# Where the last four h2 tiles are scaled: in front of the routing, or behind the item table

## The reference

```python
x = x + g1[:, None, :] * mix                       # "x1"
h = modulate(rms_norm(x, norm2_w), sh2, sc2)       # "h2"
idx, gw = grouped_route(h, w_router, router_bias)  # 2 of 32 experts a token
y = routed_experts(h, idx, gw, w_gate, w_up, w_down)
x = x + g2[:, None, :] * y
return rms_norm(x, final_norm_w)
```

## Time and profile before

| what | us |
|---|---|
| median of 3 runs | 3030.65 |
| lowest and highest of them | 3027.68 and 3041.57 |
| span of the profiled execution | 3041.9 |
| PE busy in it | 2759.4 (91%) |
| DVE busy | 2356.1 (77%) |
| ACT busy | 1565.1 (51%) |
| POOL busy | 548.3 (18%) |

### The profile page before, as it was taken

How to read it: one execution, slowest core, us unless ns; L and a number is a source line. 1 busy time by engine, 2 the same in 40 slices (tenths; PEclk the granted TensorE clock), 3 DMA queues, 4 the chain that set the end, 5 groups by cost and what they waited for, 6 DMA issues and landing times.

```text
span 3041.9 us, 34857 instructions
## 1 busy us (share of the span) xinstructions
PE 2759.4 (91%) x12582; PEld 2240.1 (74%) x12582; DVE 2356.1 (77%) x1894; ACT 1565.1 (51%) x1510; POOL 548.3 (18%) x432
## 2 busy tenths in 40 slices
PE   2799999999999788999965999999999999999992
PEld 2577777777677566788864888778888877887872
DVE  4879989987857575444445999889999888988894
ACT  6322222222122653333323877777888777777773
POOL 0000000000211110100001333222343222423230
PEclk8899999999999698999986999999999999999996
DMA  9733333334856426555536899999999999999997
GB/s 326 264 111 104 97 104 97 104 104 132 277 187 198 156 80 233 176 190 181 203 97 240 348 374 365 361 378 375 384 368 372 381 377 378 373 373 369 371 388 278
DMA packets 243520, 781.30 MB, mean 257 GB/s; under 512 B 27713, under 2 KB 122065, under 8 KB 173949
## 3 DMA queue, kind: packets, MB, share of 16 engines
q1 hardware_dynamic: 198738, 615.29, 53.0%
q0 software_dynamic: 34144, 130.08, 14.0%
q10 hardware_dynamic: 10570, 35.05, 3.0%
HBM read 738.30 MB, written 87.11 MB: 271 GB/s over the span
## 4 chain that ended last, share of the span: by engine, by line
PE 31%; DMA 12%; DVE 7%; SPq 5%; issue 4%; ACT 3%; DVEq 0%; POOL 0%; ACTq 0%; POOLq 0%
DMA wraw<-in_w_up_dram 8%; SPq L1514 4%; PE ps L1572 4%; PE ps L1570 4%; PE ps L1571 4%; PE ps L1768 3%; PE ps L1770 3%; PE ps L1769 3%; DVE wlo L1590 3%; PE ps L1870 2%; PE ps L1871 2%; PE ps L1875 2%; ACT whi L1580 2%; DMA wraw_o<-in_w_out_dram 2%; PE ps L1559 1%
## 5 line engine op out<-in xcount | busy, mean ns | idle before, releaser
L1590 DVE TENSOR_TENSOR wlo<-wraw,whi 128x2048 fp32r<-128x2048 f32 x444 | 1003.7, 2285 | 101.9 <-ACT whi L1580 101.6
L1580 ACT ACTIVATE whi<-wraw 128x2048 fp32r<-128x2048 f32 x444 | 848.2, 1918 | 311.5 <-PE ps L1572 91.3
L1570 PE MATMUL ps<-whi,xhi 128*128 128x512 f32 x1184 | 476.7, 403 | 4.5 <-DVE wlo L1590 4.4
L1572 PE MATMUL ps<-whi,xlo 128*128 128x512 f32 x1184 | 464.6, 392 | 0.0
L1571 PE MATMUL ps<-wlo,xhi 128*128 128x512 f32 x1184 | 462.9, 391 | 0.0
L715 PE MATMUL ps<-hh,wih 128*128 128x512 f32 x1056 | 336.9, 400 | 6.3 <-DVE wil L703 6.3
L715 PE MATMUL ps<-hl,wih 128*128 128x512 f32 x1056 | 330.4, 394 | 0.0
L715 PE MATMUL ps<-hh,wil 128*128 128x512 f32 x1056 | 329.9, 393 | 0.0
L1049 DVE SCALAR_TENSOR_TENSOR acc<-u,vcur,acc 128x1024 f32<-128x1024 f32 x240 | 308.3, 1284 | 8.0
L1570 PEld LDWEIGHTS ps<-whi,xhi 128*128 128x128 f32 x1184 | 224.1, 189 | 49.7 <-DVE wlo L1590 7.5
L1572 PEld LDWEIGHTS ps<-whi,xlo 128*128 128x128 f32 x1184 | 222.8, 188 | 48.6
(11 more groups left out here) (375 smaller groups left out, 4300.8 us busy)
## 6 DMA issues: line engine op xcount, KB each, us to landing
wraw<-in_w_gate_dram SPq DMA_DIRECT2D x148, 1024.0 KB, 8.5
wraw<-in_w_up_dram SPq DMA_DIRECT2D x148, 1024.0 KB, 11.8
wraw<-in_w_down_dram SPq DMA_DIRECT2D x148, 1024.0 KB, 10.9
wm<-in_w_mod_dram POOLq DMA_DIRECT2D x88, 512.0 KB, 4.1
wraw_i<-in_w_in_dram SPq DMA_DIRECT2D x72, 512.0 KB, 4.7
wraw_o<-in_w_out_dram SPq DMA_DIRECT2D x128, 256.0 KB, 3.5
wmA<-in_w_mod_dram SPq DMA_DIRECT2D x54, 512.0 KB, 5.4
u<-in_w_mod_dram POOLq DMA_DIRECT2D x24, 512.0 KB, 4.6
```

The costliest lines, as they stand in the source:

```text
L1570: pe.matmul(dst, xhi[:, t, :], whi[:, s, w], start=(t == 0), stop=False)
L1572: last = pe.matmul(dst, xlo[:, t, :], whi[:, s, w], start=False, stop=(t == KT - 1))
L1580: act.activation(whi[:, spl(m), :], wraw[:, raw(m), :], ACT.Copy).then_inc(s_whi, 1)
L1590: dve.tensor_tensor(wlo[:, spl(m), :], wraw[:, raw(m), :], whi[:, spl(m), :].bitcast(F32), ALU.subtract).then_inc(s_wsp[raw(m)], 1)
```

## The change

The four h2 scales move from in front of the routing chain to behind `itab`. POOL's adding stores of them move behind the x1 stores, the clearing of `xrow` and the bias add. SP waits for the x1 stores instead of for the h2 stores, and loads `gp` ahead of the four weight pieces instead of behind them. No instruction is added or taken away, except that SP's four waits name other semaphores.

```diff
@@ block.sync
                     load_piece(sp, 0, GATE, 0, 0)
                     load_piece(sp, 0, *STREAM[0], 1)
                     for j in range(HT, TT):
-                        sp.wait_ge(s_h2s[j], 16)
-                    for m in range(1, NRAW - 1):
-                        load_piece(sp, 0, *STREAM[m], m + 1)
+                        sp.wait_ge(s_x1[j], 16)
                     sp.wait_ge(s_h2p, 16 * HT)
                     sp.wait_ge(s_gst, 32)
                     for h, src in enumerate((modp_d[CHUNKS - 1, :, :], modg_d[:, :])):
                         sp.dma_start(gp[:, 1024 * h:1024 * h + 1024], src).then_inc(s_gp, 16)
+                    for m in range(1, NRAW - 1):
+                        load_piece(sp, 0, *STREAM[m], m + 1)
                     sp.wait_ge(s_tab, 1)
@@ block.gpsimd
-                    pool.wait_ge(s_h2p, 16 * HT)
-                    for j in range(HT, TT):
-                        pool.wait_ge(s_hs, 2 * HT + j - HT + 1)
-                        pool.dma_start(h2_d[j * P:(j + 1) * P, :], h2_tile(j), accum_op=ALU.add).then_inc(s_h2s[j], 16)
                     for j in range(HT, TT):
                         x1_store(j)
                     for j in range(TT):
                         pool.wait_ge(s_x1[j], 16)
...
                     pool.wait_ge(s_gp, 32)
                     pool.dma_start(gp[0:1, :], b_mod[:, 5 * D:6 * D], accum_op=ALU.add).then_inc(s_gb, 16)
+                    pool.wait_ge(s_h2p, 16 * HT)
+                    for j in range(HT, TT):
+                        pool.wait_ge(s_hs, 2 * HT + j - HT + 1)
+                        pool.dma_start(h2_d[j * P:(j + 1) * P, :], h2_tile(j), accum_op=ALU.add).then_inc(s_h2s[j], 16)
                     pool.wait_ge(s_its, 32)
@@ block.vector
                     bias_logits(1)
-                    for j in range(HT, TT):
-                        h2_scale(j, slice(0, D), 0)
                     dve.wait_ge(s_rex, 2)
...
                     dve.tensor_tensor(itab[:], eix[:], tmp1[:], ALU.add).then_inc(s_tab, 1)
+                    for j in range(HT, TT):
+                        h2_scale(j, slice(0, D), 0)
                     dve.wait_ge(s_ids, 1)
```

## The result

| | kernel before | changed kernel |
|---|---|---|
| median of 20 runs each | 3039.82 us | 3047.48 us |
| lowest and highest | 3027.68 and 3048.75 us | 3038.60 and 3057.72 us |
| span of the profiled execution | 3041.9 us | 3044.1 us |

The ratio is 1.0028, 95% interval 1.0017 to 1.0038: by this ratio the change makes the kernel some 8.5 us slower, while the two medians differ by 7.7 us. The forecast was +0.9 us and 3031.6 us, so the median measured lies some 16 us above it. Of these, 7 us belong to the change.

What follows compares the result with a forecast made beforehand. The prediction took PE's item loop as the bound, with only its start movable. The 8.6 us routing gain and the table's shorter queueing were given back by h2 stores on the path: net +0.9 us, 3031.6 us, range 3024 to 3041 us.

Steps and rivals of the forecast that it cites:

- What bounds the kernel: PE is busy 100 of 100 us in the item loop, so the change can only shift the loop's start, 1644.88 us.
- Part 1: The scales leave the front of the routing on DVE: routing moves up 8.6 us, `itab` ends at 1609.0 us.
- Part 2: x1 stores first: landed near 1585 us, weight pieces down by about 1600 us; clearing `xrow` costs 0 of 0 to +1.8 us.
- Part 3: SP issues the item table at 1609.05 us into empty queues; it needs 8 to 13.5 us, arriving between 1617 and 1622.5 us.
- Part 4: Scales and adding h2 stores behind the table: two adding tiles share with weight pieces, +5.0 us, last landing 1639.5 instead of 1634.5 us.
- a landing after 1643 us: Sign of a wrong forecast: h2 stores landing after 1643 us, where about 1639.5 us was expected.
- Part 5: From h2 stores to PE: index copy 0.2 us, issue step 0.4, gather 5.6; first transpose at 1645.8 us, +0.9 us.
- Rival (b): Plain weight pieces crowd out the last two adding tiles, and copy and gather run in company: +9.0 us, 3039.7 us; chance 0.13.
- Rival (a): Adding stores end undisturbed by weight pieces, at 1634.5 to 1636 us: -5 to -3 us, 3026 us; chance 0.22.
- a base of three runs: The forecast applied its change to the median of three runs of the kernel before, 3030.65 us; they differ by 14 us.
- the clock: TensorE's clock rise may fall up to 3 us to either side against PE's start, at half speed worth 1.5 us.
- The forecast of no change beyond 0.5%: Whole kernel: all cases lie inside some 0.5%, 15 us; chance 0.93 for the same, 0.03 faster, 0.04 slower.

## Why the prediction was wrong

**What bounds the kernel:** right. The change only moved the start of the loop. From the first to the last `hlo` product the loop takes 1302.9 us, against 1307.4 us before; over all kernels here that stretch lies between 1302 and 1310 us, in no order that follows the start. That is why single spans differ by less or more than the start does.

**Part 1:** right. `itab` was forecast 8.6 us earlier, and is.

**Part 2:** right here, and by luck in one term. x1 was down at 1585.6 us, and clearing `xrow` beside the routing cost it nothing:

```profile
1585.64 1.80 POOL L1710 MEMSET xrow<- 128x2048 f32 x1 [14.10 <-DMA x_d<-xb]
```

The prediction took 0 for this clearing out of 0 to 1.8 us, because DVE's scales had run at full speed beside POOL's issues, and because it took the exclusion for one of operations with two inputs against readers of SBUF. Three of the executions above paid 0.9, 1.3 and 1.7 us, with a DVE operation of one input held up by a clearing. The bound was right, the reasons were not enough, and the 0 hung on the moment at which x1 had landed.

**Part 3:** right in time (9.1 us, forecast 8 to 13.5) and wrong in what it means. The prediction saw 6 us between the emptying of the queues and the table's arrival, and took them for a latency of the table alone, off the path once the stores were later. They were writes that block what stands behind them on the same DMA engines. This is the step that failed: the table's wait was put off the path, at no cost to the adding stores. Before, nothing large stood behind the table until it had landed, so that no row showed the block; the change moved the adding stores right behind it. With `itab` at 1608.25 us the first add was to land at 1619.1 us (1619.8 less the shift of 0.75 us of the anchor), and landed at 1611.04 + 13.8 = 1624.8 us: **5.7 us** lost.

**Part 4:** the mechanism and its rate were right. Pieces sent at 1621.59 us (forecast 1621.6 with the shift), shared one for one: from 1624.8 to 1646.7 us for three adding tiles is 7.3 us each, forecast 7.4 in company. But after a late start three tiles met the pieces, not two, which is **2.2 us** more. So the last landing came at 1646.7 instead of 1638.8 us, late by 7.9 us. The prediction had named a landing after 1643 us as a sign of being wrong. The Trainium skill, DMA: Bandwidth & Descriptors, section on queues, rings and completion order, spoke against the change by each engine's turns between the queues that have work. The trace agrees: 7.3 us a tile beside the pieces, 4.9 us with the pieces held.

**Part 5:** the copy took 0.18 us, as taken. It ended just before DVE's clearing began, so it does not test the reason given; the gather's issue did stand beside that clearing and took 1.12 us. The step to the issue took 0.65 instead of 0.4 us, and the gather 4.2 instead of 5.6 us, with no piece sent between 1625.99 and 1651.20 us. Together that gives 1 us back.

In sum 0.9 + 5.7 + 2.2 - 1 = 7.8 us, against 8.0 measured. Rival (b) had almost this number, +9.0 us, by luck. Its price on the adding tiles, the whole 7.5 us of three pieces, was nearly paid (21.9 us for three tiles, against 14.7 alone), but by sharing one for one over three tiles after a late start, and not because the pieces went first. The 5.6 us that it added for a copy and a gather in company were not paid; the 5.7 us of blocked stores stand in their place. Rival (a) would have needed the pieces to be late. They were on time.

**The range** was wrong for two reasons: the blocked stores, and a base of three runs. Their own spread of 14 us was named, yet the range was widened for the clock only. It took both: about the median of twenty the same bounds, -6.9 to +10.5 us, would have held the time measured; and about the median of twenty a change of +0.9 us, 3040.7 us, would have been inside the range as it stands. The forecast of no change beyond 0.5% held; an effect of 0.28% took 20 runs on each side to see.

## What to carry to other kernels

Where a wait moves off the path, ask not only what is late next but what will be queued behind the moved transfer: a tiny store with nothing behind it costs its latency, and the same store ahead of 4 MB cost those 5.7 us as well. Store small tables so that no two values are neighbours (64 bytes apart is enough here), and read a DMA share of 1.0 together with its GB/s. And before a base is taken from three runs that differ by half a per cent, the range has to carry that half per cent.

## What the runs showed of the hardware

- 128 values of 4 bytes next to each other in DRAM took 7.4 to 9.1 us from issue until they could be read back; 64 bytes apart, or as rows of 64 or 512 bytes, 1.5 to 1.6 us. The DMA moved 33 GB/s with all engines counted busy while an adding store waited behind them (first landing 13.0 to 13.8 us instead of 7.8). The same 146 packets took 0.7% of the engines' time, so the busy time is that of the stores behind. That the writes to one small stretch wait for each other is inferred from the spacing alone; the smallest spacing that helps was not measured.
- Adding stores alone: 4.9 us a megabyte tile. Beside plain loads of another queue: 7.3 us.
- POOL's three small steps to a gather: 0.18, 0.19 and 1.1 us with DVE idle or (the last two) in its clearing, up to 2.28 and 2.13 us for the first two beside DVE's splits, and 2.98 to 5.05 us for the gather's issue. The two longest issues, 5.04 and 5.05 us, stood beside a clearing and the split behind it; why they did not end within the clearing is open. Holding the splits back brought all three to 0.18, 0.19 and 1.12 us. This agrees with the exclusion of DVE and GpSimd that the Trainium skill describes in SBUF — State Buffer, section on two separate sides; here it decided how much of an earlier table reached PE.
- It goes the other way too: a DVE operation with one input, 0.29 us alone, took 1.20 to 2.01 us beside POOL's clearing of `xrow` (1.80 us) in three executions, by the moment at which the two met.
